# One encoder layer on one core: x loaded in the order of the turned tokens, the second pair of x tiles normed ahead of the parameters, constants fed to TensorE in its waits, expert 0's rows weighted later, the S5 matrix B built one chunk earlier

## The chip, the cores and the metric

One NeuronCore of a Trainium2 chip. Its engines run side by side and wait for each other by semaphores: TensorE (PE; its weight load is PEld), VectorE (DVE), ScalarE (ACT), GpSimd (POOL) and SyncE (SP), which here only issues DMAs; ACT and POOL issue some too. The metric is the device time of one execution in microseconds, the lower the better; the values of before are three runs.

## The reference

One layer over 512 tokens (an 8 x 64 grid) of width 1024, all float32:

```python
h = rms_norm(x, norm_mix)                      # x (512, 1024)
q, k, v, u, q_xa, gates = split(h @ w_in)      # w_in (1024, 5120)
x = x + (sum_b sigmoid(gate_b) * P_b(branch_b)) @ w_out
#   neighbourhood attention, 8 heads, 8 x 16 window on the grid, learned bias
#   bidirectional S5 scan (16 groups x 16 channels, 64 states), GELU, GLU
#   4-head cross-attention into 256 memory tokens, normed and projected
h2 = rms_norm(x, norm_ffn)
x = x + moe(h2)      # 4 groups x 4 experts, top-1 group, top-2 experts in it, FF 256
return rms_norm(x, final_norm)
```

The S5 step needs B-bar times the powers of the state's decay for each lag within a block of 8 tokens; before calls this ba. A token's two experts weight their outputs with softmax(top 2) times the group's probability.

## The kernel before

**Precision.** A product of two float32 matrices is three fp32r products: each operand is split into hi (rounded copy) and lo (rest), and `split()` (lines 1533 to 1537) adds hi x hi, lo x hi and hi x lo. A weight chunk arrives in `raw`, ScalarE writes w_hi (`hi`, L560), VectorE w_lo = raw - w_hi (`lo`, L962), then TensorE may take it. `RAW` = 6 raw buffers, `HL` = 2 pairs of w_hi and w_lo.

**Queues.** Each engine's program is written out in its own block and runs in order. SP issues every weight load in order of chunks; a load of chunk c waits until w_lo of chunk c - 6 is done.

**The opening.** SP loads x in four tiles of 128 tokens in natural order (L432), then chunk 0, the parameters (rows of the tile prm, L445, and the log step, L454), chunk 1, mem, chunks 2 and 3. ScalarE first loads its table for the square root (L571), then squares each tile with a sum (L574); after each pair the roots. VectorE turns them into 1/rms (`inverse_root`) and scales the tiles (`norm_x`, L970). TensorE transposes the normed tiles block by block (`turn`, L1557): eight blocks b of 128 columns, each block's 512 tokens in one PSUM bank, `TURN_BANK`. Blocks 0 to 5 are turned in two halves, (0, 1) and (2, 3), blocks 6 and 7 whole, after blocks 0 and 1 have left their banks. Between the halves stands `turn_params` (L1543), which turns prm into per-partition columns prt (the norm's gains among them); VectorE prepares prm for it (L977), after all eight parameter transfers, before it goes on to the second pair. From prt on, ScalarE writes h_hi = gain x block (`turn_hi`, L585) and VectorE h_lo (`turn_lo`, L988). The tokens are kept in another order from here on, column within the grid before row, so that both write with a stride of eight elements what they read in runs. The later load of x for the residual (L494) and the last sums already use that order: `every_eighth` writes 16 partitions, eight apart, of all four tiles, one transfer for each of the eight grid rows.

**Projection and branches.** Chunks c = 0 to 52 follow, with one to four products each (`product`), on banks 0 and 1 in turn. Chunks 0 and 1 give u of S5, 2 and 3 the cross-attention's queries, 4 to 7 the keys and values of mem, 8 to 19 q, k, v, 20 to 52 gates and branch projections. Work of the branches stands between the chunks on each engine at hand-placed values of c. On VectorE: `disc`, `powers` and `bbar` (c = 1 to 3) prepare B-bar, and `forward_b(h)`, called at c = 6 and 7 behind w_lo of chunk c + 2, multiplies it by powers for half of the states: four multiplies of 128 x 512 (L1078 to L1081; banks 2, 3 and 7, junk) and two sums into ba (L1083). `v_take` (L1195) copies turned values, for chunk 8 those of the memory (vm). TensorE turns values between the chunks (`turn_values`, L1670: the second of them, behind chunk 8's product, waits for v_take of the first), and ba from c = 9 on. GpSimd builds ba's other direction meanwhile.

**Routing and experts.** After w_out, the logits of the last tiles end on TensorE as products of 20 columns. VectorE picks groups and experts (`chosen`), TensorE sums their one-hots to places (`places`, L1847), VectorE builds one-hot tiles for the first `NHOT` = 4 experts, TensorE turns each into row numbers (L1859), and GpSimd gathers the rows of h2 by them into xg (L2148). For all experts GpSimd scatters token numbers and weights into tok_scratch (L2163, eight transfers), reads them back as idx (L2171) and copies each expert's weights to wcur (L2175); from expert 4 on it gathers by idx. `tokens(e)` (L1871) turns xg, `gate_up` multiplies by the gate and up weights in two halves, and the next step multiplies by the down weights (products `e_hi, at_hi`). An expert's weights are three units of 1 MB; ScalarE splits e_hi (`unit_hi`, L799), VectorE e_lo (L1413). ScalarE takes expert e - 1's output times its tokens' weights to ysb (`y_take(e)`, L855), which waits for wcur, and GpSimd adds it to the accumulator in DRAM (`add_y`, L413). For expert 0 ScalarE's y_take(1) stands in step 2, between unit 8's split and the tanh of expert 2; TensorE's down product of step 2 waits for it.

## Time and profile before

| | |
|---|---|
| runs of before (us) | 639.74, 641.40, 640.41; median 640.41 |
| profiled execution | 639.83 us, its span 638.2 us, mean granted clock 0.965 |
| PE busy in the span | 588.4 us (92%) |
| DVE, ACT, POOL busy | 416.5 (65%), 324.3 (51%), 221.4 (35%) us |

PE is busy in nearly all of the 40 slices of the page; the exceptions are the first and second, the end, and two around 450 and 485 us, where also the granted clock of TensorE is below 1 on average:

```profile
PE   2899799999999999999999999997497999999992
PEclk9899899999999999999999999997597999999997
```

Each digit is a slice of 16 us in tenths. A granted clock of 1.00 is 2.4 GHz, one of 0.50 is 1.2 GHz. In a timeline a matmul's duration counts until its end is modelled; the pace of a stream is the difference of two starts, or the length in the chain.

### The profile page before, as it was taken

The numbers are of one execution on the slowest core, as the hardware profiler recorded it, in microseconds if no ns is written. First come the engines' busy times: TensorE is split into PE (matmuls) and PEld (weight loads), VectorE is DVE, ScalarE is ACT, GpSimd is POOL, SyncE is SP. The second block draws the span as 40 slices with busy tenths as digits, with TensorE's granted clock in tenths as the row PEclk, the third lists the DMA queues.
The fourth block names the chain that finished last, engine by engine and source line by source line (L and its number), as shares of the span: only waits on it lengthen the run. The fifth ranks groups of instructions, "written<-read, shape, count | busy, mean of one in ns | idle before, by whom it ended". The sixth has DMA issues, their size and how long they took to land.

```text
span 638.2 us, 8989 instructions
## 1 busy us (share of the span) xinstructions
PE 588.4 (92%) x3149; PEld 477.0 (75%) x3149; DVE 416.5 (65%) x744; ACT 324.3 (51%) x533; POOL 221.4 (35%) x235
## 2 busy tenths in 40 slices
PE   2899799999999999999999999997497999999992
PEld 2688688889877777777677888887376888888871
DVE  3977523695376664554842379324877899999967
ACT  5866133222344433553243326315175998998853
POOL 3507985995000810000000000023665345434930
PEclk9899899999999999999999999997597999999997
DMA  9994523420253222222322336973599999999355
GB/s 299 197 217 115 116 68 101 126 72 1 63 169 88 78 66 67 67 67 66 100 65 67 100 99 155 334 275 132 158 324 405 374 365 393 399 386 374 130 108 199
DMA packets 89232, 111.46 MB, mean 175 GB/s; under 512 B 19647, under 2 KB 66913, under 8 KB 89192
## 3 DMA queue, kind: packets, MB, share of 16 engines
q1 hardware_dynamic: 79128, 93.65, 45.2%
q0 software_dynamic: 7280, 15.12, 8.7%
q10 hardware_dynamic: 2784, 2.18, 1.2%
q8 instruction: 23, 0.38, 0.2%
q14 instruction: 17, 0.14, 0.1%
HBM read 102.08 MB, written 14.75 MB: 183 GB/s over the span
## 4 chain that ended last, share of the span: by engine, by line
PE 77%; DVE 7%; DMA 5%; issue 4%; SPq 2%; POOL 2%; ACT 1%; POOLq 0%; ACTq 0%; DVEq 0%
PE bank L1535 21%; PE bank L1537 20%; PE bank L1536 20%; PE bank L1716 2%; PE bank L1690 2%; PE bank L1703 2%; DMA acc_scratch<-ysb,idx 2%; PE bank L1871 2%; DMA tok_scratch<-pay,rowi 1%; PE bank L1821 1%; SPq L483 1%; PE bank L1651 1%; DVE w_lo L962 1%; POOL tok_scratch L2163 1%; PE bank L1655 1%
## 5 line engine op out<-in xcount | busy, mean ns | idle before, releaser
L962 DVE TENSOR_TENSOR w_lo<-raw,w_hi 128x1024 fp32r<-128x1024 f32 x55 | 73.2, 1331 | 110.0 <-ACT w_hi L560 109.5
L1535 PE MATMUL bank<-h_hi,w_hi 128*128 128x512 f32 x320 | 129.6, 405 | 0.3 <-DVE w_lo L962 0.3
L1537 PE MATMUL bank<-h_hi,w_lo 128*128 128x512 f32 x320 | 126.1, 394 | 0.0
L1536 PE MATMUL bank<-h_lo,w_hi 128*128 128x512 f32 x320 | 125.6, 393 | 0.0
L1413 DVE TENSOR_TENSOR e_lo<-eraw,e_hi 128x2048 fp32r<-128x2048 f32 x48 | 108.7, 2291 | 8.9 <-ACT e_hi L799 7.6
L799 ACT CAST e_hi<-eraw 128x2048 fp32r<-128x2048 f32 x48 | 91.8, 1915 | 10.6 <-PE bank L1537 6.4
L560 ACT CAST w_hi<-raw 128x1024 fp32r<-128x1024 f32 x55 | 57.6, 1047 | 33.8 <-PE bank L1537 33.6
L1535 PEld LDWEIGHTS bank<-h_hi,w_hi 128*128 128x128 f32 x320 | 61.0, 191 | 13.1 <-DVE w_lo L962 0.9
L1537 PEld LDWEIGHTS bank<-h_hi,w_lo 128*128 128x128 f32 x320 | 60.6, 189 | 13.4
L1536 PEld LDWEIGHTS bank<-h_lo,w_hi 128*128 128x128 f32 x320 | 61.0, 191 | 11.7
L2113 POOL TENSOR_TENSOR wcf<-wcf,prt 128x160 f32<-128x160 f32 x1 | 0.5, 458 | 194.9 <-DMA wcf<-in_moe_w_fine 194.9
L1535 PE MATMUL bank<-e_hi,xt_hi 128*128 128x512 f32 x128 | 52.7, 412 | 1.6 <-DVE e_lo L1413 1.0
L1536 PE MATMUL bank<-e_lo,xt_hi 128*128 128x512 f32 x128 | 51.0, 398 | 0.0
L1537 PE MATMUL bank<-e_hi,xt_lo 128*128 128x512 f32 x128 | 51.0, 398 | 0.0
L413 POOL DMA_INDIRECT acc_scratch<-ysb,idx x14 | 25.6, 1831 | 56.8 <-PE bank L1871 41.6
L659 ACT ACTIVATE gt<-bank,bgh 128x512 f32<-128x512 f32 x24 | 16.5, 689 | 43.5 <-PE bank L1537 43.5
L2148 POOL DMA_INDIRECT xg<-h_scratch,idx x16 | 30.1, 1881 | 11.5 <-DVE idx L1408 8.6
L673 ACT ACTIVATE pr<-ssb,soft 128x192 f32<-128x192 f32 (+1 forms) x32 | 15.2, 475 | 30.2 <-DVE soft L1223 30.2
L1535 PE MATMUL bank<-e_hi,at_hi 128*128 128x512 f32 x64 | 26.1, 407 | 4.7 <-ACT ysb L855 3.7
L1535 PEld LDWEIGHTS bank<-e_hi,xt_hi 128*128 128x128 f32 x128 | 24.8, 193 | 7.3 <-DVE e_lo L1413 1.0
L1537 PEld LDWEIGHTS bank<-e_hi,xt_lo 128*128 128x128 f32 x128 | 24.6, 193 | 5.4
L1536 PEld LDWEIGHTS bank<-e_lo,xt_hi 128*128 128x128 f32 x128 | 24.8, 194 | 4.7
(390 smaller groups left out, 1228.5 us busy)
## 6 DMA issues: line engine op xcount, KB each, us to landing
raw<-in_w_in SPq DMA_DIRECT2D x40, 512.0 KB, 3.9
eraw<-in_moe_w_gate SPq DMA_DIRECT2D x32, 512.0 KB
eraw<-in_moe_w_up SPq DMA_DIRECT2D x32, 512.0 KB
eraw<-in_moe_w_down SPq DMA_DIRECT2D x32, 512.0 KB
raw<-in_w_out SPq DMA_DIRECT2D x8, 512.0 KB, 3.8
x_sb<-in_x SPq DMA_DIRECT2D x4, 512.0 KB, 5.0
raw<-in_w_mem_kv SPq DMA_DIRECT2D x4, 512.0 KB, 9.8
raw<-in_w_br_na SPq DMA_DIRECT2D x4, 512.0 KB, 3.4
```

The source lines that it names most:

```text
L413: pool.indirect_dma_start(out=acc_dram, out_offset=bass.IndirectOffsetOnAxis(ap=v(idx, 2 * e, [1, 1]), axis=0), in_=v(ysb, D * (e % 2), [1 ...
L560: act.copy(v(dst, o, [1, 1024]), v(raw, 1024 * (c % RAW), [1, 1024])).then_inc(sem("w_hi_done"), 1)
L659: ins = act.activation(v(gt, SEQ * m, [1, SEQ]), pv(g % 2, 0, [1, SEQ]), ACT.Tanh, scale=0.5, bias=v(bgh, KD * branch + m, [1, 1]))
L673: ins = act.activation(v(pr, 512 * (p % 2) + 256 * j, [1, n]), src, ACT.Exp, bias=v(soft, so + 1, [1, 1]), accum_out=v(soft, so + 2, [1, 1]))
L799: act.copy(v(e_hi[dst], 0, [1, 2048]), v(eraw[j], 0, [1, 2048])).then_inc(sem("e_hi_done"), 1)
L962: dve.tensor_tensor(v(l_, o, [1, 1024]), v(raw, 1024 * (c % RAW), [1, 1024]), raw32(v(h_, o, [1, 1024])), SUB).then_inc(sem("w_lo_done"), 1)
L1413: dve.tensor_tensor(v(e_lo[dst], 0, [1, 2048]), v(eraw[j], 0, [1, 2048]), raw32(v(e_hi[dst], 0, [1, 2048])), SUB).then_inc(sem("e_lo_done" ...
L1535: pe.matmul(dst, w[0], x[0], start=first, stop=False)
L1536: pe.matmul(dst, w[0], x[1], start=False, stop=False)
L1537: return pe.matmul(dst, w[1], x[0], start=False, stop=last)
L1690: ins = pe.matmul(pv(2 + j, 0, [1, n]), x, y, start=True, stop=True)
L2148: pool.indirect_dma_start(out=v(xg, D * (e % 3), [1, D]), out_offset=None, in_=h2_dram, in_offset=bass.IndirectOffsetOnAxis(ap=rows, axis= ...
```

## The change

x is loaded by 16 transfers of 128 KB, each of one grid row (16 partitions, eight apart) of two tiles: the even rows on SP, the odd rows on ACT ahead of everything else there, first those of tiles 0 and 1, then of 2 and 3. So tokens lie in their later order from the start and `turn_hi`, `turn_lo` read and write in runs; a square waits for all eight transfers of its pair. VectorE norms the second pair before it waits for the parameters. TensorE turns seven blocks of the first pair, then the same of the second, then the parameters, and waits for prt; block 6 has a bank of its own (bank 1), and only block 7 waits for a bank. `warm(b, n)` issues n bf16 products of a constant 128 x 128 by 512 columns into bank b, whose results nobody reads: 2 and 6 in the opening, 12 before `chosen`, (8, 0, 12, 1) ahead of the four one-hot tiles, 12 ahead of the first gathered rows, 3 behind their turning. y_take(1) takes expert 0's output unweighted and doesn't wait for wcur; `y_first`, in step 2 ahead of y_take(2), multiplies it in place, and add_y(0) waits for that. forward_b moves from c = 6, 7 to c = 5, 6.

```diff
 # loads, tile order
-        for n in range(NT):
-            sp.dma_start(v(x_sb, D * n, [1, D]), x_nat[:, n, :]).then_inc(sem(f"x_in{n}"), 16)
+        for n in (0, 2):
+            for r in range(0, ROWS, 2):
+                sp.dma_start(every_eighth(x_sb, r, n, 2), x_rows[:, n:n + 2, r, :]).then_inc(sem(f"x_in{n}"), 16)
...
+        for n in (0, 2):
+            for r in range(1, ROWS, 2):
+                act.dma_start(every_eighth(x_sb, r, n, 2), x_rows[:, n:n + 2, r, :]).then_inc(sem(f"x_in{n}"), 16)
         act.wait_ge(sem("stat_set"), 1)
         act.activation(v(stat, 40, [1, 1]), v(stat, 48, [1, 1]), ACT.Sqrt)
         for n in range(NT):
-            act.wait_ge(sem(f"x_in{n}"), 16)
+            if n % 2 == 0:
+                act.wait_ge(sem(f"x_in{n}"), 16 * ROWS)
...
-    TURN_BANK = (4, 5, 6, 7, 2, 3, 4, 5) + 2 * (4, 5, 6, 7)
+    TURN_BANK = (4, 5, 6, 7, 2, 3, 1, 4) + 2 * (4, 5, 6, 7)
...
-                act.activation(v(h_hi, SEQ * b, [1, ROWS], [ROWS, GW]), pv(TURN_BANK[b], 0, [GW, ROWS], [1, GW]),
-                               ACT.Identity, scale=pcol(GMIX + b)).then_inc(sem("turn_hi"), 1)
+                act.activation(v(h_hi, SEQ * b, [1, SEQ]), pv(TURN_BANK[b], 0, [1, SEQ]), ACT.Identity, scale=pcol(GMIX + b)).then_inc(sem("turn_hi"), 1)
...
         norm_x(0)
         norm_x(1)
+        inverse_root(2, 2, 2)
+        norm_x(2)
+        norm_x(3)
         dve.wait_ge(sem("prm_in"), 16 * 8)
         done(dve.tensor_copy(v(prm, 0, [64, 2], [1, 64], p0=LDT, pn=DP),
                              v(stat, 60, [1, 2], [0, 64], p0=LDT, pn=DP)), "prm_ready")
-        inverse_root(2, 2, 2)
-        norm_x(2)
-        norm_x(3)
...
         for b in range(6):
             turn(b, (0, 1))
+        turn(6, (0, 1))
+        warm(0, 2)
+        for b in range(7):
+            turn(b, (2, 3))
         turn_params()
-        for b in range(6):
-            turn(b, (2, 3))
-        for b in range(6, KD):
-            turn(b, (0, 1, 2, 3))
+        pe.wait_ge(sem("prt_ready"), 1)
+        warm(0, 6)
+        turn(7, (0, 1, 2, 3))
 # B
-            if c in (6, 7):
+            if c in (5, 6):
                 dve.wait_ge(sem("ct_ready"), 2)
-                forward_b(c - 6)
-            if c == 7:
+                forward_b(c - 5)
+            if c == 6:
                 dve.sem_inc(sem("ba_ready"), 1)
 # constants
+        def warm(b, n):
+            for _ in range(n):
+                pe.matmul(pv(b, 0, [1, 512]), v(onesb, 0, [1, P]), v(onesb, 0, [0, 4], [1, P]), start=True, stop=True)
...
         logits(3)
+        warm(0, 12)
         pe.wait_ge(sem("chosen"), 1)
...
         for e in range(NHOT):
+            warm(0, (8, 0, 12, 1)[e])
             pe.wait_ge(sem("hot"), e + 1)
...
+        warm(0, 12)
         pe.wait_ge(sem("rows"), 1)
         tokens(0, 0, 16)
+        warm(0, 3)
 # expert 0's rows
-            act.wait_ge(sem("wcur"), e)
+            plain = isinstance(e, int) and e == 1
+            if not plain:
+                act.wait_ge(sem("wcur"), e)
...
-                                     ACT.Identity, scale=v(wcur, 0 if odd else 1, [1, 1]))
+                                     ACT.Identity, scale=1.0 if plain else v(wcur, 0 if odd else 1, [1, 1]))
...
+        def y_first():
+            act.wait_ge(sem("y_a"), 1)
+            act.wait_ge(sem("wcur"), 1)
+            act.mul(v(ysb, 0, [1, D]), v(ysb, 0, [1, D]), v(wcur, 0, [1, 1])).then_inc(sem("y_first"), 1)
```

## Rows read from the trace of the kernel before

**Rows 1.** timeline, 0 to 22 us: start, us, engine, operation, line, [idle before <-releaser]

```profile
0.93 1.28 ACT L571 ACT_TABLE_LOAD   x1 [0.93 <-PEq L2228]
...
4.33 1.06 ACT L574 ACTIVATE squares<-x_sb 128x1024 f32<-128x1024 f32 x1 [1.90 <-DMA x_sb<-in_x]
...
9.51 2.79 PE L1557 MATMUL bank<-ident,x_sb 128*128 128x128 f32 x12 [9.51 <-DVE x_sb L970]
...
12.13 0.22 DVE L977 COPY prm<-stat 16x128 f32<-16x128 f32 x1 [2.76 <-DMA stat<-in_s_log_dt]
...
14.71 1.53 PE L1557 MATMUL bank<-ident,x_sb 128*128 128x128 f32 x12 [1.89 <-DVE x_sb L970]
14.86 1.23 DVE L962 TENSOR_TENSOR w_lo<-raw,w_hi 128x1024 fp32r<-128x1024 f32 x1
15.25 7.87 ACT L585 ACTIVATE h_hi<-bank,prt 128x512 fp32r<-128x512 f32 x8 [3.64 <-PE bank L1557]
...
16.50 6.47 DVE L988 SCALAR_TENSOR_TENSOR h_lo<-bank,prt,h_hi 128x512 fp32r<-128x512 f32 x6 [0.42 <-ACT h_hi L585]
```

**Rows 2.** timeline, TensorE, around the second product and around 71 us

```profile
26.46 0.50 PE L1535 MATMUL bank<-h_hi,w_hi 128*128 128x512 f32 x1
...
71.24 0.66 PE L1670 MATMUL bank<-ident,vt 128*128 128x128 f32 x2 [3.87 <-DVE vm L1195]
```

**Rows 3.** timeline, VectorE, 54 to 73 us

```profile
55.03 1.85 DVE L962 TENSOR_TENSOR w_lo<-raw,w_hi 128x1024 fp32r<-128x1024 f32 x1 [0.20 <-ACT w_hi L560]
59.59 1.96 DVE L962 TENSOR_TENSOR w_lo<-raw,w_hi 128x1024 fp32r<-128x1024 f32 x1 [2.72 <-ACT w_hi L560]
61.48 0.68 DVE L1078 TENSOR_TENSOR bank<-pw,bank 128x512 f32<-128x512 f32 x1
...
65.30 1.51 DVE L962 TENSOR_TENSOR w_lo<-raw,w_hi 128x1024 fp32r<-128x1024 f32 x1
...
70.67 0.42 DVE L1195 COPY vm<-bank 128x256 f32<-128x256 f32 x1 [0.15 <-DVE ba L1083]
```

**Rows 4.** waits of TensorE, whole span: waiter <- releaser: total us, times, longest

```profile
PE bank L1859 <- DVE hot L1401: 5.6, 4, 2.8
```

**Rows 5.** timeline, routing and first experts

```profile
445.82 0.23 PE L1847 MATMUL bank<-selb,upper 128*128 128x64 bf16 x1 [2.88 <-DVE selb L1381]
...
455.78 1.94 PE L1871 MATMUL bank<-ident,xg 128*128 128x128 f32 x8 [2.90 <-DMA xg<-h_scratch,idx]
...
487.23 1.06 POOL L2148 DMA_INDIRECT xg<-h_scratch,idx  x1 [0.15 <-issue]
...
488.46 0.76 PE L1535 MATMUL bank<-e_hi,at_hi 128*128 128x512 f32 x1 [3.66 <-ACT ysb L855]
...
496.91 1.05 PE L1871 MATMUL bank<-ident,xg 128*128 128x128 f32 x8
```

**Rows 6.** windows: us, busy us of each engine, granted clock, DMA share, GB/s

```profile
3.50:8.50 5.00, 0.00 (x0) 0.00 (x0) 1.40 (x6) 3.51 (x6) 3.32 (x6) 1.00 0.98 362
391.00:401.00 10.00, 10.00 (x46) 8.28 (x45) 7.89 (x8) 6.49 (x8) 0.00 (x0) 1.00 1.01 235
442.00:444.00 2.00, 0.94 (x5) 0.83 (x4) 0.98 (x8) 1.98 (x2) 0.00 (x1) 0.50 0.67 270
490.00:492.00 2.00, 2.00 (x6) 1.52 (x5) 1.59 (x1) 0.37 (x1) 2.00 (x2) 0.50 1.04 414
```

**Rows 7.** chain that ended last, around 72 us: start, us, what

```profile
72.33 0.43 PE bank L1536
...
75.40 0.23 PE bank L1536
```

**Rows 8.** instructions on tile x_sb, the later load: ns min/median/max

```profile
L494 SPq DMA_DIRECT2D x_sb<-in_x x8: 580/595/701, 390.1 to 394.7; - x8
```

**Rows 9.** groups by line and form, VectorE, 100 to 360: busy us, mean ns

```profile
L1183 DVE SCALAR_TENSOR_TENSOR merged<-gt,bank 128x512 f32<-128x512 f32 x8 | 5.5, 684 | 3.5 <-PE bank L1537 3.3 <-DVE merged L1183 0.2
```

**Rows 10.** DMA queues, 492 to 493 us: packets, MB, share of 16 engines

```profile
q0 software_dynamic: 85, 0.09, 25.6%
```

More of the change, by code:

```diff
@@ L129, in v, with every_eighth @@
         return bass.AP(tensor=first.tensor, offset=first.offset + off, ap=[first.ap[0]] + [list(d) for d in dims])
-    def every_eighth(t, r):
+    def every_eighth(t, r, n0=0, nn=NT):
         first = t[r:r + 1, 0:1]
-        return bass.AP(tensor=first.tensor, offset=first.offset, ap=[[ROWS * first.ap[0][0], P // ROWS], [D, NT], [1, D]])
+        return bass.AP(tensor=first.tensor, offset=first.offset + D * n0,
+                       ap=[[ROWS * first.ap[0][0], P // ROWS], [D, nn], [1, D]])
     def spread(t, r, cols):
@@ L284, in build @@
     x_rows = a["x"][0].rearrange("(r n c) d -> c n r d", r=ROWS, n=NT)
-    x_nat = a["x"][0].rearrange("(n p) d -> p n d", p=P)
     out_nat = out[0].rearrange("(n p) d -> p n d", p=P)
@@ L406, in add_y @@
     def add_y(pool, e):
-        pool.wait_ge(sem("y_a"), e + 1)
+        if e == 0:
+            pool.wait_ge(sem("y_first"), 1)
+        else:
+            pool.wait_ge(sem("y_a"), e + 1)
         if e == 0:
@@ L894, in step @@
             elif not peeled or 2 <= e < 15:
+                if peeled and e == 2:
+                    y_first()
                 y_take(e, odd)
@@ L986, in turn_lo @@
             if b < KD:
-                o = [[1, ROWS], [ROWS, GW]]
-                dve.scalar_tensor_tensor(v(h_lo, SEQ * b, *o), pv(TURN_BANK[b], 0, [GW, ROWS], [1, GW]),
-                                         pcol(GMIX + b), raw32(v(h_hi, SEQ * b, *o)), MUL, SUB).then_inc(
+                dve.scalar_tensor_tensor(v(h_lo, SEQ * b, [1, SEQ]), pv(TURN_BANK[b], 0, [1, SEQ]),
+                                         pcol(GMIX + b), raw32(v(h_hi, SEQ * b, [1, SEQ])), MUL, SUB).then_inc(
                                              sem("turn_lo"), 1)
@@ L1510, in last_sum @@
             dve.wait_ge(sem("out_k"), NT + n + 1)
-            dve.wait_ge(sem(f"x_in{n}"), 48)
+            dve.wait_ge(sem(f"x_in{n}"), 32 if n % 2 else 32 + 16 * ROWS)
             for b in range(2):
@@ L1549, in turn @@
                 pe.wait_ge(sem("normed"), tiles[-1] + 1)
-                if b >= 6:
-                    pe.wait_ge(sem("turn_lo"), b - 5)
+                if b == 7:
+                    pe.wait_ge(sem("turn_lo"), 1)
             else:
```

## The prediction

> **What bounds the kernel now.** I read the waits of TensorE first, then the order of time around each, then the windows and the chain. Outside three places TensorE hardly waits, so the change pays only there. The first is the opening: TensorE's first instruction stands at 9.51, because x has to land, be squared and be normed; the second pair of x tiles is then held up by VectorE, which waits 2.76 us for the parameters; and from 15.25 on ScalarE and VectorE take eight turned blocks out of PSUM, 7.87 us for eight and 6.47 for six [rows 1], before w_lo of chunk 1 and the second product at 26.46 [rows 2]. The second is one stall: at 71.24 TensorE has idled 3.87 us for VectorE's copy of vm [rows 2], which stood behind forward_b [rows 3]. The third is routing with the first experts, where TensorE waits 5.6 us in four pieces for the one-hot tiles [rows 4], 2.88 for the chosen experts, 2.90 for the first gathered rows and 3.66 for ScalarE's ysb [rows 5]. After such a stretch the granted clock is 0.50 (1.2 GHz) for a while, as at 442 to 444 and 490 to 492 [rows 6]; products then follow each other every 0.43 us and not every 0.23 [rows 7].
>
> **Opening: x by 16 transfers, second pair ahead of the parameters.** Removed: the 2.76 us wait. Added: 12 more DMA issues, eight of them on ScalarE ahead of its table load. An issue of this kind, for a transfer twice as big, took 0.595 us [rows 8]; the bounds for one are 0 and 0.7, and I take 0.6. So ScalarE issues until 0.93 + 8 x 0.6 = 5.7 and, with the table load of 1.28 [rows 1] and the small root of 0.2 (an estimate), squares from 7.2, not from 4.33. First pair: 2.9 late, first transpose at 12.4 instead of 9.51.
>
> Landing: each new transfer writes 16 partitions eight apart. The nearest rows are the later loads of x of the same form, 235 GB/s for the core while they ran, against 362 in the opening now [rows 6]. Half a MB at 362 is 1.45 us and the first tile was in use at 4.33, so 2.9 us go beside the data. 2.1 MB at 235 is 8.9: second pair there at 11.8. From first square to first transpose it took 9.51 - 4.33 = 5.2, so transposes of the second pair start at 17.0, not at 14.71 [rows 1]. Fourteen of them now stand ahead of the parameters' transpose: 14 x 0.13 (12 took 1.53) = 1.8, then 0.7 for it and its copy (an estimate): prt is ready at 19.5 and h_hi starts 4.2 us later than at 15.25.
>
> What comes back is the eviction. The block in PSUM is now in its final order, so it is written contiguously; VectorE's nearest instruction of that size takes 0.68 [rows 9] against 6.47 / 6 = 1.08. VectorE: w_lo of chunk 0 1.2, eight h_lo 5.4, w_lo of chunk 1 1.2, end 27.3. TensorE: six constants, block 7 at 21.5, then 24 x 0.23 = 5.5 us of first product, end 27.5. The second product starts there and not at 26.46: **1.0 us lost**. From the other side: with loads at full rate ScalarE binds (first pair squared at 9.7, transposes of the second at 14.9), the end is 25.2 and 1.2 are gained; with 0.23 a transpose in both pairs (the first twelve took 2.79) and 3.4 us of the first product at half speed, 4.1 are lost. I stay at 1.0, since the form of the transfer is that of the 235 row. SP issues the parameters about 3 us later, behind eight transfers instead of four; they were there at 12.1, so about 15, in time for the norm's end at about 17. The chunks and mem behind them shift as far, hidden while ScalarE is on h_hi, which even now it leaves only at 23.1.
>
> The Trainium skill, page SBUF — State Buffer, section Door 1: The DMA port swizzle, says that a transfer reaches only the ports its partitions map to, all 16 only if it spans all 128. By its formula the partitions of one new transfer lie on 8 ports, an estimate of 218 GB/s, by which 1.7 us would be lost in place of 1.0; the 235 measured agrees roughly.
>
> **B one chunk earlier.** forward_b's instructions are only moved, from behind chunks 6 and 7 to behind 5 and 6. w_lo of chunk 7 ends at 55.03 + 1.85 = 56.9; forward_b takes 65.30 - 61.48 = 3.8, to 60.7; w_lo of chunk 8 1.7 (between 1.51 and 1.96), to 62.4 instead of 61.55 [rows 3]. So product 8 starts 0.9 late and ends at 68.3 (now 71.24 - 3.87 = 67.4). The second half runs to 66.2, w_lo of chunk 9 to 67.7, vm is copied by 68.1: just in time. TensorE goes on at 68.3 in place of 71.24, 2.9 less. With the idle time the half clock goes too: six products at 0.43 instead of 0.23 [rows 7] and two transposes of 0.66 in place of 0.25 [rows 2], 1.6. Together **4.5 gained**; 2.9 if the clock falls anyway, 0 if vm waits as before (rival 6). Behind it TensorE waits for next to nothing as far as 400 us, so it is kept. Late next is w_lo of chunk 8.
>
> **Constants in routing.** They stand in order on TensorE, so each group is free only if it ends before that which it is put ahead of. No row shows a bf16 product of 512 columns; the nearest are the products of 512 at 0.23 and 0.43. Twelve start at 445.82 - 2.88 = 442.9 [rows 5], the clock at 0.50 [rows 6]. At full speed 12 x 0.23 = 2.8 us just fill the wait; at half they take 5.2 and end 2.3 late. Near 72 us the clock came back after about 3.4 us of unbroken work: 72.33 is slow, 75.40 fast [rows 7]. So eight slow and four fast, end 447.3, 1.5 late, part of which VectorE's own work hides. The next 8 + 12 + 1 are 4.8 us against 5.6 of waits [rows 4], the last 12 2.8 against 2.90. I take 1.2 us of delay for all that hangs on routing: 0 if it never runs at half, 8 in rival 5. In return the first experts' products run at 0.23: twelve save 2.4, of which VectorE's e_lo, next to be late, leaves about 1.6.
>
> **First rows weighted later.** The 3.66 us wait for ysb goes, and the slow stretch behind it (0.50 at 490 to 492 [rows 6]), 13 products, 2.6. ScalarE takes the rows as soon as it has split unit 8, for which TensorE still waits about 1.3; y_first adds a 1024-column multiply before the next take (1.06 by the squares' row), hidden. Late next is the gather for expert 4: issued at 487.23 [rows 5], behind the arrival of idx, which this edit doesn't move, and now behind 1.2 us of constants. GpSimd's queue was still moving bytes at 492 to 493 [rows 10]; I put its landing at 493.3 now and 494.6 after. TensorE would be ready at about 492, and turns the rows at 494.6 in place of 496.91 [rows 5]: 2.3 gained, less 0.7 for a chance of 4 in 10 that 2.7 us of idling halve the clock for 3.4 us (1.7). **1.6 gained.** Bounds: if the gather lands only at 496.5 now, 2.6 are lost (0.9 late, 1.7 clock); if it is never late, 5.0 are gained.
>
> **Sum.** +1.0 - 4.5 - 1.6 = -5.1. The profiled execution took 639.83 (638.2 of span, 1.6 around it), so 634.7; it lies 0.6 under the median of the runs, so 635.3.
>
> **Rivals.**
> 1. The gather of expert 4 is early and the experts gain 5.0 instead of 1.6: 631.9. For: no row shows its landing. Against: the queue's late bytes. 0.15.
> 2. That gather gives the gain back, +2.6 in place of -1.6: 639.5. For: the core's DMA is full of weights there. 0.19.
> 3. The opening costs 4.1 and not 1.0: 638.4. For: the second pair then falls on slow transposes. Against: the constants. 0.10.
> 4. The opening gains 1.2: 633.1. For: the 235 stands for a stretch with other transfers in it. 0.11.
> 5. Slower: the constants never lift the clock, so 12, 8, 12, 1 and 12 of them run at 0.43. The places come 2.3 us late; 21 more take 9.0 against 5.6 of waits, the last 12 5.2 against 2.9: about 8 us on the first gathered rows and on the chain to idx, in place of 1.6 gained: 644.9. It decides if the granted clock is still 0.50 behind the first twelve. Against: near 72 us unbroken work brought it back. 0.05.
> 6. B earlier doesn't do what it says: vm still waits, behind a stretched w_lo, and 4.5 shrinks to 0: 639.8. Against: forward_b is the only work between. 0.04.
>
> The forecast has 0.36 (its own range 633.2 to 637.5). What a measurement can't tell from no change is within 0.3%, 1.9 us, of 640.41. Faster: forecast, 1, 4, two thirds of 3, a third of 2: 0.75. Same: 6 and most of the rest of 2 and 3: 0.18. Slower: 5 and a tail of 2: 0.07. Range 631.0 to 640.3.
>
> **What would show it.** Opening: first square near 7.2, second pair landed near 11.8, h_hi from 19.5 at 0.6 each, second product near 27.4. Middle: no idling above 2 us between 58 and 75, granted clock 1.00 there. Routing: clock 1.00 within 4 us of the first constants, first gathered rows turned about 1.2 late. Experts: waits for ysb under 2 us and a new wait for the gather of expert 4. I am wrong above all if x lands whole by 9 us, if the one-hots wait for constants, or if that gather comes later than 496.

## The result: 651.0 us, slower than before

| | us |
|---|---|
| before, 5 runs | 639.74 to 642.72, median 640.41 |
| after, 5 runs | 643.81 to 654.89, median 651.0 |
| ratio of after to before | 1.013, 95% interval 1.0085 to 1.0174 |
| predicted | 635.3 (631.0 to 640.3) |
| after's profiled execution | 643.81, span 642.2, granted clock 0.983 |

The forecast had the wrong sign. The ratios, here and below, leave out runs that are over 1.5% above the fastest of their kernel, as they may be in a slower state of the chip (here 654.89). The runs spread over 11 us and the profiled execution is the fastest of the five, so its trace shows only part of the loss. On the page TensorE's row is better than before at the first weak place (9 for 4) and its clock row at both (9 for 5 and for 7), yet the chain that ended last no longer runs over TensorE alone:

```profile
PE   1898999999999999999999999999987999999980
...
PEclk9999999999999999999999999997999999999995
...
PE 54%; DMA 21%; DVE 10%; issue 6%; ACT 3%; POOL 3%; SPq 2%; POOLq 0%; ACTq 0%; DVEq 0%
DMA acc_scratch<-ysb,idx 17%; PE bank L1550 14%; PE bank L1552 13%; PE bank L1551 13%; DVE w_lo L978 2%; PE bank L1736 2%; PE bank L1723 2%; PE bank L1710 2%; DMA xg<-h_scratch,idx 1%; POOL tok_scratch L2190 1%; PE bank L1671 1%; PE bank L1
```

Before, that chain was 77% PE, and the transfer `acc_scratch<-ysb,idx`, by which GpSimd adds an expert's output to the accumulator in DRAM, had 2% of it. It has 17% now.

**Up to expert 4 it goes much as forecast.** The opening in the timeline of after (start, duration, engine, line, operation; answers to [rows 1]):

```profile
0.94 5.18 ACTq L576 DMA_DIRECT2D x_sb<-in_x  x8
...
8.19 1.06 ACT L582 ACTIVATE squares<-x_sb 128x1024 f32<-128x1024 f32 x1 [0.55 <-DMA x_sb<-in_x]
...
12.86 1.06 ACT L582 ACTIVATE squares<-x_sb 128x1024 f32<-128x1024 f32 x1 [2.15 <-DMA x_sb<-in_x]
...
17.67 1.75 PE L1577 MATMUL bank<-ident,x_sb 128*128 128x128 f32 x14 [1.09 <-DVE x_sb L986]
...
19.91 4.74 ACT L593 ACTIVATE h_hi<-bank,prt 128x512 fp32r<-128x512 f32 x8 [3.60 <-DVE prt L999]
...
21.06 5.36 DVE L1003 SCALAR_TENSOR_TENSOR h_lo<-bank,prt,h_hi 128x512 fp32r<-128x512 f32 x8
```

ScalarE issues for 5.18 us, the first square stands at 8.19, h_hi starts at 19.91 and takes 0.59 a block, h_lo 0.67 [rows 1, 9]. The second product starts at 27.88, 1.42 late. While x was loaded, the core moved 223 GB/s (last number of the window), where before moved 362:

```profile
3.50:8.50 5.00, 0.00 (x0) 0.00 (x0) 0.00 (x0) 1.80 (x3) 3.32 (x6) 1.00 1.00 223
```

The middle and the S5 outputs on TensorE (answers to [rows 2]):

```profile
70.06 0.41 PE L1690 MATMUL bank<-ident,vt 128*128 128x128 f32 x2 [0.23 <-DVE vm L1210]
...
147.50 0.49 PE L1671 MATMUL bank<-st_re,ca 128*128 128x128 f32 x2 [0.84 <-DVE st_im L1147]
```

The wait for vm is 0.23 us and the granted clock 1.00 from 55 to 80. At 80 us after is 2.63 us ahead. At 147.50 TensorE waits for S5's state, which VectorE doesn't have earlier; 1.1 us go back there.

Routing and the first experts on TensorE (answers to [rows 5]), then three windows of after (us, busy of each engine, granted clock, DMA share, GB/s):

```profile
440.44 5.29 PE L1558 MATMUL bank<-onesb 128*128 128x512 bf16 x12
...
454.93 1.14 PE L1896 MATMUL bank<-ident,xg 128*128 128x128 f32 x8
...
478.87 1.16 PE L1896 MATMUL bank<-ident,xg 128*128 128x128 f32 x8 [1.36 <-DMA xg<-h_scratch,idx]
...
483.68 0.47 PE L1550 MATMUL bank<-e_hi,at_hi 128*128 128x512 f32 x1 [0.90 <-ACT ysb L864]
...
492.08 1.15 PE L1896 MATMUL bank<-ident,xg 128*128 128x128 f32 x8 [2.45 <-DMA xg<-h_scratch,idx]
```

```profile
441.00:446.00 5.00, 5.00 (x21) 1.91 (x19) 3.27 (x19) 1.98 (x3) 0.00 (x0) 0.51 0.26 105
446.00:452.00 6.00, 5.25 (x36) 2.29 (x35) 5.76 (x13) 0.00 (x0) 2.24 (x1) 1.00 0.00 0
484.00:488.00 4.00, 4.00 (x19) 3.29 (x18) 3.90 (x4) 2.83 (x2) 2.11 (x3) 1.00 1.03 411
```

The first twelve constants all ran at the half clock, 5.29 us for twelve, and only behind them the granted clock is back at 1.00. TensorE came to the places at 445.51; VectorE had written the chosen experts (selb) by 443.4. The stall for ysb is 0.90 in place of 3.66, and tokens(4) waits 2.45 us for its gather: 492.08 in place of 496.91, 4.8 us ahead of before.

**Behind that, everything is given back.** ScalarE around the first add of after, then the first and the twelfth add on GpSimd:

```profile
482.45 1.09 ACT L864 ACTIVATE ysb<-bank 128x512 f32<-128x512 f32 x2
...
488.59 1.15 ACT L871 ACTIVATE ysb<-ysb,wcur 128x1024 f32<-128x1024 f32 x1
```

```profile
490.55 2.00 POOL L416 DMA_INDIRECT acc_scratch<-ysb,idx  x1 [4.29 <-ACT ysb L871]
...
596.48 2.81 POOL L416 DMA_INDIRECT acc_scratch<-ysb,idx  x1 [4.86 <-DMA acc_scratch<-ysb,idx]
```

The same two adds, the first and the last steady one, of before:

```profile
489.13 1.67 POOL L413 DMA_INDIRECT acc_scratch<-ysb,idx  x1 [0.84 <-ACT ysb L855]
...
591.22 2.00 POOL L413 DMA_INDIRECT acc_scratch<-ysb,idx  x1 [5.92 <-DMA acc_scratch<-ysb,idx]
```

y_take(1) runs at 482.45, but y_first stands behind the splits of two units, at 488.59, and the first add waits for it: 490.55, where before had 489.13. From there the chain of after is one add behind the other (start, length, what):

```profile
490.55 9.12 DMA acc_scratch<-ysb,idx
...
500.53 8.73 DMA acc_scratch<-ysb,idx
...
510.11 8.65 DMA acc_scratch<-ysb,idx
```

An add waits until the one before has landed. How GpSimd came to its 14 adds, first before, then after (durations of the issue in ns, min/median/max; idle us and times by what ended them):

```profile
L413 POOL DMA_INDIRECT acc_scratch<-ysb,idx x14: 1577/1724/2196, 489.1 to 611.6; - x14
...
  PE bank L1871: 41.6, 9
  DMA acc_scratch<-ysb,idx: 14.2, 3
```

```profile
L416 POOL DMA_INDIRECT acc_scratch<-ysb,idx x14: 1577/2186/3554, 490.6 to 615.5; - x14
...
  DMA acc_scratch<-ysb,idx: 63.8, 12
```

Before, TensorE's progress released nine of the fourteen adds and a landing three. After, the landing of the add before released twelve. Eleven steps from 490.55 to 596.48 are 9.63 us each, against TensorE's own 9.31 an expert; before they were (591.22 - 489.13) / 11 = 9.28. So the last steady add is 5.3 us late, 1.4 by its start and 3.8 by the pace. Of that the tail gives some back and takes some more: the next add follows after 10.8 us and not 14.2, but its issue takes 3.49 us, not 1.62. The loads of the accumulated rows, which wait for the adds, start 4.0 us late, first before, then after, and that is the difference of the two spans:

```profile
616.94 4.98 SPq L545 DMA_DIRECT2D xf<-acc_scratch  x8
```

```profile
620.91 4.99 SPq L549 DMA_DIRECT2D xf<-acc_scratch  x8
```

TensorE was not what came late: at the last `tokens` of this stretch it still led before by 1.0 us (598.26 against 599.28). It had lost 3.8 of its 4.8 us, as GpSimd's program has, for each expert, a copy to wcur, the gather for a later expert and one add in turn, so that late adds hold up gathers: between 484 and 606 TensorE waits three times for gathered rows, 3.8 us with the 2.45 above, in before not once.

### The profile page after: what moved, and what is told of

It reads as the page before. It is cut to its first block, busy times and chain, and to the rows that moved or that the text cites. A ratio compares the mean times of both kernels' runs of the same rounds, so it can differ in the third digit from the quotient of the medians.

```text
span 642.2 us, 9113 instructions
## 1 busy us (share of the span) xinstructions
PE 594.9 (93%) x3205; PEld 475.4 (74%) x3205; DVE 414.4 (65%) x744; ACT 321.7 (50%) x534; POOL 213.4 (33%) x235
## 4 chain that ended last, share of the span: by engine, by line
PE 54%; DMA 21%; DVE 10%; issue 6%; ACT 3%; POOL 3%; SPq 2%; POOLq 0%; ACTq 0%; DVEq 0%
DMA acc_scratch<-ysb,idx 17%; PE bank L1550 14%; PE bank L1552 13%; PE bank L1551 13%; DVE w_lo L978 2%; PE bank L1736 2%; PE bank L1723 2%; PE bank L1710 2%; DMA xg<-h_scratch,idx 1%; POOL tok_scratch L2190 1%; PE bank L1671 1%; PE bank L1844 1%; SPq L487 1%; DMA x_sb<-in_x 1%; PE bank L1558 1%
## 5 line engine op out<-in xcount | busy, mean ns | idle before, releaser
L978 DVE TENSOR_TENSOR w_lo<-raw,w_hi 128x1024 fp32r<-128x1024 f32 x55 | 74.7, 1358 | 106.2 <-ACT w_hi L564 105.5
L1550 PE MATMUL bank<-h_hi,w_hi 128*128 128x512 f32 x320 | 128.2, 401 | 1.6 <-DVE w_lo L978 1.6
L416 POOL DMA_INDIRECT acc_scratch<-ysb,idx x14 | 33.0, 2359 | 68.2 <-DMA acc_scratch<-ysb,idx 63.8
L854 ACT CAST xt_hi<-bank 128x512 fp32r<-128x512 f32 x32 | 17.2, 591 | 20.6 <-PE bank L1896 20.4
```

Of the source, the lines that this page charges most:

```text
L416: pool.indirect_dma_start(out=acc_dram, out_offset=bass.IndirectOffsetOnAxis(ap=v(idx, 2 * e, [1, 1]), axis=0), in_=v(ysb, D * (e % 2), [1 ...
L854: act.copy(v(xt_hi[odd], 512 * j, [1, 512]), pv(4 + j, 0, [1, 512])).then_inc(sem("xt_hi"), 1)
L978: dve.tensor_tensor(v(l_, o, [1, 1024]), v(raw, 1024 * (c % RAW), [1, 1024]), raw32(v(h_, o, [1, 1024])), SUB).then_inc(sem("w_lo_done"), 1)
L1550: pe.matmul(dst, w[0], x[0], start=first, stop=False)
```

## Experiments

Theory: expert 0's late weighting sets off a serial chain of adds that was at its limit already. Each kernel was compared with runs of before on the same chip (medians 640.8 to 641.6); "ratio" is to those, with its 95% interval. "Less than after" is against its median of 651.0; a second series of after (after_again, below) had 648.36, which makes each such difference 2.6 us smaller.

### Undoing y_first, moving it, breaking the chain

**a_weighted**: after, with

```diff
-            plain = isinstance(e, int) and e == 1
-            if not plain:
-                act.wait_ge(sem("wcur"), e)
+            act.wait_ge(sem("wcur"), e)
...
-                if peeled and e == 2:
-                    y_first()
```

`scale` and add_y's wait are as in before again, too.

> After with one part undone: y_take(1) weights expert 0's rows again and waits for wcur, y_first is gone. Theory (chain of adds): the adds to the accumulator run one after the other, each 8.8 us to landing and 0.86 to the next start, which is more than TensorE's 9.31 us per expert, so the last steady add stands at the first plus 11 x 9.6 and the end follows it. Here the first add moves from 490.55 to about 486.5 (wcur at 484.3, two takes of 0.6, the start of the DMA), TensorE stalls 2 us more at about 484: end 4 us earlier than after's profiled 643.8, about 640. Rival 1 (the loss of after sits before the experts, in the opening or the constants): no change but the stall, 645 to 648. Rival 2 (the DMA engines are full in the experts, so every period is 9.6 whatever starts when): within 1 us of 643.8 or later.

Measured 639.04, ratio 0.9954 (0.9932 to 0.9976): 12 us less than after by taking one part out. The stall is back (3.7 us for ysb); the first add stands at 486.84.

**a_two_acc**: after, with odd adds to a second tensor. The kernel leaves the rows of that tensor out of its output, so it is a probe and no candidate; the waits of y_take and of the last loads, not shown, follow the two semaphores.

```diff
-        pool.indirect_dma_start(out=acc_dram,
+        pool.indirect_dma_start(out=acc2_dram if e % 2 else acc_dram,
...
-            pool.wait_ge(sem("y_acc"), 16 * e)
+            pool.wait_ge(sem(("y_acc", "acc_set")[e % 2]), 16 * (e // 2) + (48 if e % 2 else 0))
```

> After, with the adds of the odd experts sent to a second DRAM tensor (filled from x beforehand), so that each add waits only for the last but one; the second tensor is left out of the output. Theory (chain of adds): TensorE runs at its own 9.31 us per expert from tokens(4) at 492.08, the last steady add at about 586.5 in place of 596.48: 10 us less, about 634, and the spread of the runs falls to that of before (3 us). Rival (DMA engines full): the period stays at 9.6 and the time within 2 us of after's 643.8. Rival (only the phase of GpSimd's descriptors against VectorE counts): the adds still take 2.2 us to issue, but without a chain this costs nothing, so it would look as under the theory; the issue times tell it apart.

Measured 635.61 (635.21 to 637.23), 0.9906 (0.9878 to 0.9934): 15 us less than after, and the spread is 2 us. The DMA engines are as busy as ever (share 1.00 from 500 to 600, 0.98 in after), so it was not their fill. Steady adds now follow each other every 9.31 us, though each takes 2.1 to issue.

**a_early**: after, with y_first one unit earlier.

```diff
                 unit_hi(3 * e + 3, (n0 + 1) % EU, load_of(n0 + 1, i), 0)
+                if peeled and e == 2:
+                    y_first()
                 unit_hi(3 * e + 4, (n0 + 2) % EU, load_of(n0 + 2, i), 1)
```

> After, with y_first placed behind the split of unit 9 and not behind that of unit 10, 3 us earlier on ScalarE. Theory (chain of adds): the first add moves from 490.55 to about 487.6, every later add with it, TensorE unchanged until tokens(4): 3 us less than 643.8, about 641. Rivals (loss before the experts; DMA engines full): no change, 643 to 645.

Measured 642.14, 1.0000 (0.9973 to 1.0026). More than the 3 us came back, yet it is 3 us slower than a_weighted, though both start alike. First and last steady add on GpSimd, of a_weighted and of a_early:

```profile
486.84 1.67 POOL L413 DMA_INDIRECT acc_scratch<-ysb,idx  x1 [0.83 <-ACT ysb L859]
...
587.66 2.09 POOL L413 DMA_INDIRECT acc_scratch<-ysb,idx  x1 [3.65 <-ACT ysb L859]
```

```profile
486.98 2.00 POOL L416 DMA_INDIRECT acc_scratch<-ysb,idx  x1 [1.21 <-ACT ysb L871]
...
595.99 2.23 POOL L416 DMA_INDIRECT acc_scratch<-ysb,idx  x1 [5.08 <-DMA acc_scratch<-ysb,idx]
```

Steps of 9.17 there, 9.91 here. So the start is not all. In a_weighted TensorE has lost 3.7 us to the stall and turns expert 4's rows at 493.47, in a_early at 491.59: the same adds stand further behind TensorE in a_early, and twelve adds wait for a landing, where in a_weighted five do. That a landing releases the adds doesn't make them slow by itself: it releases twelve in the profiles of b_B, b_open, b_const and b_split too, with steps of 9.39 to 9.50. What counts is how long a step is, and the next part takes it to pieces.

**b_yfirst**: before, with y_first alone (the part of the change as in its diff).

> Before, with the one part: expert 0's rows taken unweighted, weighted by y_first ahead of y_take(2). Theory (chain of adds): TensorE's stall of 3.66 us goes, but y_first stands some 6 us behind y_take(1), so the first add moves from 489.13 to about 492; with adds back to back at 9.6 the end comes 3 (TensorE's pace kept) to 7 us later: 643 to 647. As I predicted for this part: 1.6 us gained, 638.8. Rival (loss sits in the opening or the constants): between 636 and 640.

Measured 655.04, 1.0191 (1.0155 to 1.0227): by itself this part costs 12 us by the ratio and 13.5 by the medians, more than the theory's 7 and, by the medians, more than the whole change (the intervals of the two ratios overlap). Its first ten steps are 9.3 to 12.5 us.

### Why the steps get longer

VectorE and GpSimd around the fifth add of after:

```profile
528.64 4.49 DVE L1428 TENSOR_TENSOR e_lo<-eraw,e_hi 128x2048 fp32r<-128x2048 f32 x2
```

```profile
528.84 3.55 POOL L416 DMA_INDIRECT acc_scratch<-ysb,idx  x1 [5.10 <-DMA acc_scratch<-ysb,idx]
```

The two e_lo run from 528.64 to 530.93 and from 530.84 to 533.13. The issue of the add starts 0.2 us into the first and ends at 532.39, 1.46 behind that one's end. The same 1.46 to 1.48 us stand behind the end of a running e_lo in ten other adds of after and in seven of before; where none runs at its start, the issue takes 1.58 to 1.67, also beside VectorE's instructions that read a PSUM bank. The Trainium skill, page SBUF — State Buffer, section SBUF: two separate sides, states that VectorE and GpSimd share a port pair by an exclusive lock held for a whole instruction, and that a VectorE instruction with two SBUF inputs, as e_lo is, takes it against a GpSimd instruction that reads SBUF. The trace agrees that GpSimd waits for the end of e_lo; it adds that 1.46 us of the issue still lie behind it. What exactly of the issue is held up no run shows. In a_weighted the issues take 1.59 us each from 496 to 532 and 2.1 from 541 on, where TensorE paces them; in after, where each starts by the landing of the one before, they take 1.7 to 3.6.

A step is the issue, the rest of the transfer up to its landing, and the time to the next add. Summed over the eleven steps from the first add to the last steady one (us, from rows like those above; the runs not yet named follow below):

| | issues | issue's end to landing | landing to next add | eleven steps |
|---|---|---|---|---|
| before | 20.4 | 71.6 | 10.1 | 102.1 |
| after | 25.2 | 71.5 | 9.3 | 105.9 |
| after_again | 26.6 | 71.3 | 9.3 | 107.1 |
| a_late_pe | 23.2 | 70.9 | 9.3 | 103.4 |
| a_esplit | 24.3 | 72.7 | 9.3 | 106.3 |
| b_B | 24.5 | 70.1 | 9.3 | 103.9 |
| b_yfirst | 27.8 | 75.4 | 9.3 | 112.6 |
| a_oldopen | 27.5 | 79.0 | 9.3 | 115.7 |

In the two profiles of after the transfers take what they took before; the longer issues, 4.7 and 6.1 us, more than make up the slower pace, 3.8 and 5.0. In b_yfirst and a_oldopen the transfers are longer too.

**a_late_pe**: after, with more work on TensorE.

```diff
         for e in range(3):
             step(e)
+            if e == 2:
+                warm(7, 24)
```

> After, with 24 more constants (5.5 us of work that nobody reads) on TensorE behind step 2; nothing else. The first add stays at 490.55, tokens(4) comes about 3 us later than 492.08. Theory (chain of adds and its phase): the issue of an add ends 1.46 us after VectorE's running e_lo (2.29 us) ends, so adds that start by the landing of the one before, wherever VectorE is, take 2.4 us to issue, and adds that TensorE paces take 1.6 to 2.1; with TensorE later the adds are paced by it again, each step falls from 9.6 to 9.3, the last steady add stands near 592 in place of 596.5 and the kernel gets 3 to 5 us faster than after (651.0 median), 646 to 648, although it has 5.5 us more work. Rival (chain alone, no phase): the adds keep 9.6 and the time is after's, 650 to 652. Rival (TensorE's work is what counts): 3 us slower, 654.

Measured 643.45, 1.0027 (1.0003 to 1.0052): 7.5 us less than after. The 24 products and tokens(4) on TensorE, then the last steady add:

```profile
486.37 5.35 PE L1558 MATMUL bank<-onesb 128*128 128x512 bf16 x24
...
494.52 1.05 PE L1896 MATMUL bank<-ident,xg 128*128 128x128 f32 x8
```

```profile
593.75 2.35 POOL L416 DMA_INDIRECT acc_scratch<-ysb,idx  x1 [2.30 <-DMA acc_scratch<-ysb,idx]
```

The adds stayed a chain of landings (twelve waits of 36.6 us in all, 63.8 in after), with a shorter step, 9.40, most of it by shorter issues (23.2 in place of 25.2 us). Against after_again's median the gain is 4.9 us. That 5.35 us of useless work make the kernel faster speaks against TensorE's own work as the cause; that TensorE took over the pace was wrong.

**a_esplit**: after, with shorter instructions on VectorE.

```diff
-            dve.tensor_tensor(v(e_lo[dst], 0, [1, 2048]), v(eraw[j], 0, [1, 2048]),
-                              raw32(v(e_hi[dst], 0, [1, 2048])), SUB).then_inc(sem("e_lo_done"), 1)
+            for o in (0, 1024):
+                ins = dve.tensor_tensor(v(e_lo[dst], o, [1, 1024]), v(eraw[j], o, [1, 1024]),
+                                        raw32(v(e_hi[dst], o, [1, 1024])), SUB)
+            ins.then_inc(sem("e_lo_done"), 1)
```

> After, with each e_lo (128 x 2048 on VectorE, 2.29 us) made by two instructions of 1024 columns. Theory (phase): an add's issue then waits for at most 1.2 us of a running instruction instead of 2.29; the issues fall from 2.35 us in the mean to 1.9 or less, the chain's step by 0.45, eleven steps 5 us: about 646 against 651. Rival (the issue's length has nothing to do with VectorE's instruction): issues stay at 2.35 and the time at 651, or 0.2 us more per expert where VectorE is the bound: 653.

Measured 638.85, 0.9946 (0.9918 to 0.9975): 12 us less than after, but not as worked out. The issues fell only to 2.23 in the mean (after: 2.36; the median rose from 2.19 to 2.26), the steps of the profiled execution stayed at 9.66, and the first add came 2.8 us earlier. That is most of what the two profiled executions differ by (640.46 and 643.81); the rest of the 12 us no trace shows. GpSimd got to the gather of expert 3 at 466.10, not 469.37, and through the copies to wcur by 479.1, not 485.1; TensorE and ScalarE were then 2.7 us ahead, and with them y_first (485.83, not 488.59). So what shortens is GpSimd's way through the routing. **b_split** shows the same, before with this edit alone:

> Before with e_lo by two instructions of 1024 columns alone. Theory (GpSimd's work waits for VectorE's running instruction, in the scatters, in the copies to wcur and in the adds): the first add moves 2 to 3 us forward, as from 484.37 to 481.70 with B and the constants, the late adds get shorter: 3 to 5 us less than before, 0.993 to 0.995. Rival (the split only helps a kernel whose TensorE is ahead): 1.000.

Measured 635.32 (634.52 to 638.55), 0.9918 (0.9890 to 0.9946). The third and fourth scatter of token numbers, before and b_split:

```profile
459.03 3.08 POOL L2163 DMA_INDIRECT tok_scratch<-pay,rowi  x1 [0.30 <-issue]
462.41 1.90 POOL L2163 DMA_INDIRECT tok_scratch<-pay,rowi  x1 [0.30 <-issue]
```

```profile
459.88 0.97 POOL L2165 DMA_INDIRECT tok_scratch<-pay,rowi  x1 [0.31 <-issue]
461.15 1.96 POOL L2165 DMA_INDIRECT tok_scratch<-pay,rowi  x1 [0.30 <-issue]
```

A scatter that meets no e_lo takes 0.97. The first add moves from 489.13 to 486.38; the steps get no shorter (9.39, before 9.28). So the gain is in the way to the first add and, 2.1 us, behind the last steady one.

**b_two_acc**: before, with a_two_acc's edit.

> Before, with the adds of the odd experts sent to a second DRAM tensor that is left out of the output. Theory (in before TensorE sets the pace, and the adds, 8.3 us to landing and 0.86, have only 0.16 us of room): hardly faster, 0 to 1.5 us below before (640.9), with a smaller spread. Rival (the chain of adds bound before too): over 4 us faster, as in the changed kernel, where it gave 15 us.

Measured 636.16, 0.9921 (0.9893 to 0.9949), 4.7 us less: the rival's number. So the chain of adds bounds before too, in part, and my 0.16 us of room were none. Before's profiled execution has three adds that waited for a landing; its longer runs (up to 649.7 beside this one) may have more, which no trace of before shows. b_const, below, which is as fast as before in the median, has twelve in a profiled execution of 645.02.

### The other parts

**b_B**: before with `if c in (5, 6)`, `forward_b(c - 5)` alone.

> Before, with forward_b at c = 5, 6 alone. TensorE's start of product 8's successors at 80 us is 3.9 us earlier in after than the opening alone would have it (1.25 late at 40 us, 2.63 early at 80 us). Theory (chain of adds): the adds' chain starts from the routing, so it moves with everything else; nothing is taken back: 3.9 us less than before, a ratio of 0.994. Rival: the wait for S5's state at 147 us, which took 1.1 us back in after, belongs to this part: 2.8 us less, 0.9956. Rival (the DMA queue sets the end whatever starts when): 1.000.

637.51, 0.9938 (0.9915 to 0.9962). The interval holds both numbers. By the trace the rival is right on the place: a wait of 0.7 us for S5's state is in it.

**b_open**: before with the opening alone.

> Before, with after's opening alone (x by 16 transfers, second pair ahead of the parameters, contiguous evictions, the 8 constants of the opening). From after's trace: second product at 27.88 in place of 26.46, 1.25 us late at 40 us, kept to the end: ratio 1.002. As I predicted for it: 1.0 us late. Rival (the opening is what made after slow, by later parameters): over 3 us, 1.005 and more.

643.03, 1.0048 (1.0019 to 1.0077), 2.2 us by the medians, 3.1 by the ratio; the interval does not decide between 1.3 and the rival's 3.

**b_const**: before with the constants in routing alone.

> Before, with the constants in routing and ahead of the first experts alone. Theory (chain of adds): the first add hangs on chosen, the scatter and idx, which the constants make about 0.5 us later (idx came 1.9 us earlier in after's routing than before where the logits ended 2.4 earlier); TensorE gains some 3 us in experts 0 to 2 and gives them back in the wait for ysb, which grows from 3.7 to over 5: end 0 to 1 us later, 1.000 to 1.0015. Rival (constants gain what TensorE shows at tokens(1), 2.8 us): 0.9955. Rival (constants are after's loss): 1.005 and more.

641.24, 1.0003 (0.9983 to 1.0023), as expected. The profiled execution was a long one, 645.02.

**c_Bconst**: before with B earlier and the constants.

> Before, with B one chunk earlier and the constants, without the opening and without y_first. Theory: 3.9 gained and 0.5 lost: 3.4 us less than before, 0.9947, first add at about 485.7. Rival (constants gain too): 0.990. Rival (only together do parts lose, by the phase in which the adds meet VectorE's splits): 1.000 and more, with adds whose issue takes over 2 us.

637.33, 0.9950 (0.9925 to 0.9975), as expected: it beats both kernels, by B alone. Its first add stood at 484.37, 1.3 earlier than expected.

**a_oldopen**: after without its opening.

> After without its opening (before's loads, norms and evictions of x), with B earlier, the constants and y_first. The opening alone cost 1.0048 of before on its own. Theory: its cost adds up with the rest, so 2 to 3 us less than after: 648 to 649, still slower than before. Rival (the opening makes the loss, by the moment at which everything meets GpSimd): 641 or less.

647.41, 1.0081 (1.0046 to 1.0116). The parts add up roughly. Its profiled execution, 652.26, was one of its longest (the fastest took 642.13) and shows what a single bad one looks like (chain, start and length of adds):

```profile
508.55 11.02 DMA acc_scratch<-ysb,idx
...
520.42 8.96 DMA acc_scratch<-ysb,idx
...
530.22 10.28 DMA acc_scratch<-ysb,idx
```

**after_again**: after, unchanged.

> After, unchanged, to see by another profile where the 7 us go by which its median (651.0) stands above the profiled execution (643.8). Theory (chain of adds and its phase): the first add stands at 490 to 491 again and the steps between adds are longer, 10 us and more, with issues of 2.5 to 3.5 us; the time stays near 651. Rival (the extra time lies before the experts): the first add is late.

648.36 (644.28 to 652.59), 1.0124 (1.0079 to 1.0169). The profiled execution took 645.19, again one of the fastest, with the first add at 490.12 and steps of 9.74, so the question stayed open: no profile shows after at 651. Its steps are 0.1 us longer than those of the execution at 643.81, all of it in the issues, and a_oldopen's bad execution has steps of 10.5; both point to the steps between adds, and neither shows it for after.

**c_split**: c_Bconst with e_lo in two.

> Before, with B one chunk earlier, the routing constants and e_lo by two instructions of 1024 columns: a candidate for the fastest. In the version without the split (637.3) TensorE paces most adds, so the theory gives it little: 0 to 1.5 us less (the late adds, those of 2.1 to 2.2 us, get shorter), 636 to 637.3. Rival (VectorE becomes the bound with 0.1 to 0.2 us more per expert): 638 to 640.

632.26 (630.90 to 632.79), 0.9847 (0.9811 to 0.9882): 8.5 us below before, the fastest here, and 4 to 5 us better than expected. First add, then TensorE's tokens(4) and (5), then VectorE in a steady stretch:

```profile
481.70 1.67 POOL L413 DMA_INDIRECT acc_scratch<-ysb,idx  x1 [0.30 <-issue]
```

```profile
487.38 1.15 PE L1880 MATMUL bank<-ident,xg 128*128 128x128 f32 x8 [0.69 <-DMA xg<-h_scratch,idx]
...
496.79 1.05 PE L1880 MATMUL bank<-ident,xg 128*128 128x128 f32 x8
```

```profile
540.00:590.00 50.00, 50.00 (x249) 41.96 (x248) 49.34 (x60) 45.01 (x49) 25.38 (x18) 1.00 1.01 376
```

The first add stands 7.4 us ahead of before's, and the steps are 9.09 us, with issues of 1.59 in the next five adds, all released by landings. VectorE is busy for 49.34 of 50 us: the dearer split didn't bind yet, but it is at its end.

## Why the prediction was wrong

- **Opening, 1.0 lost.** Right in mechanism, 1.4 in size: first square 8.19 (predicted 7.2), second pair squared from 12.86 (11.8), transposes 17.67 (17.0), h_hi 19.91 (19.5), second product 27.88 (27.4). x came at 223 GB/s, where 235 had been taken, and ScalarE's issues took 0.65 each, not 0.6. Alone the opening cost 2.2 by the medians.
- **B, 4.5 gained.** 3.9 at 80 us (from 1.25 late to 2.63 early), of which 1.1 went back at 147 us. "Behind it TensorE waits for next to nothing" was read from waits of a TensorE that came later; an engine that is not waited for in before can be late for one that arrives earlier. The kernel with B alone has -3.4 by the medians.
- **Constants, 1.2 of delay and a fast clock behind.** "Eight slow and four fast" was wrong: all twelve ran at 0.43 us each, the granted clock was 0.50 up to 445.7 and 1.00 from 446 on, over 5 us behind the first of them and not within 4. The places came 2.1 us late; tokens(0) came 0.85 early where 2.4 of lead had come into routing, so 1.5 of delay were left. That this is near 1.2 is in part luck. Rival 5 is false, but its first step, twelve constants at the half clock, came true: the clock rose just behind them, and the next 8 took 1.93 us, the next 12 2.75.
- **The gather of expert 4 next.** It was late by 2.45 us, as argued; tokens(4) came 4.8 ahead of before, where my steps gave 5.8 (4.5 for B and 2.3 here, less 1.0).
- **The step that failed** is one clause: "y_first adds a 1024-column multiply before the next take (1.06 by the squares' row), hidden." It is hidden from ScalarE and TensorE, and the first add stands right behind it. I asked what is late next for TensorE only, and took the period of 9.31 behind expert 4 as given. GpSimd's rows would have spoken: 8.2 us from issue to landing in the median, about 0.86 to the next issue, so 9.1 of 9.31, with three adds already released by a landing. In after the late first add is 1.4 of the 5.3 us by which the last steady add is late, the longer steps are 3.8. No rival held it; that the gain was "given back" stood only for a gather. Nor would the three signs named as "wrong above all" have told: x was whole at 12.8, the one-hots waited at most 0.4 us for constants, expert 4's rows were turned at 492.08. All three watch what TensorE needs. Without this step the forecast's other terms give -3.5; the kernel without it, a_weighted, measured -2.5 by the medians.
- The size: after is 7 to 11 us above before; y_first gives 12 to 13.5 (a_weighted, b_yfirst), the opening 2.2, the constants 0.4, B -3.4. These sum to 11 to 13, so the parts add up only roughly.

**Open.** Why one execution's steps are 9.6 and another's over 10: in a_oldopen's the transfer itself, behind the issue, takes 7.0 to 8.6 us in ten of eleven steps, where before's takes 6.1 to 7.5. No run here tells what it meets there; b_yfirst, which lost more than the theory's 7 us, has longer transfers too. Nor does a run set only the place at which the adds meet e_lo: that this place makes the issues long is shown add by add, that a lag behind TensorE leads to the bad places is argued from a_early and a_late_pe. Why the spread falls so far in c_split is only argued: its adds have some room again.

## What to carry to other kernels

When an edit takes a wait from the engine that bounds the kernel, follow what else hung on that wait: list every serial chain beside it (issue, landing, restart) and divide its step by the period; one at 98% of it is a second bound, and what starts it must not move back. If GpSimd is in such a chain, look at VectorE's instruction lengths before looking at GpSimd. And where runs spread over 11 us, one profile is a sample and can be the fastest of them: don't take what it shows for the whole difference.

## What the runs showed of the hardware

- GpSimd's indirect add takes 1.59 us to issue when no e_lo runs at its start, and up to 3.68 when it starts in an e_lo of 2.29 us (585.24 in a_early): it ends 1.46 to 1.48 us behind that e_lo. VectorE's instructions that read a PSUM bank don't hold it up (517.85 in before: 1.59, in an xt_lo). Scatters take 0.97 and up to 3.08. Halving the e_lo instructions took 5 us from before (b_split), though VectorE got no less work.
- An add of up to 128 rows of 4 KB to DRAM landed 7.7 to 9.7 us after its start beside weight loads in before (DMA share 1.03 from 540 to 590), up to 11.7 in b_yfirst, and 5.2 to 5.4 in before's tail without them. The Trainium skill, page DMA: Bandwidth & Descriptors, section Two DMAs through the same engine are not ordered, says that only the completion semaphore orders dependent transfers; this kernel keeps to it, and the price beside the loads was 8.5 (c_split) to 12.5 us (b_yfirst) per link.
- x by 16 transfers of 16 partitions each was whole for the first pair by about 8.1 us and for the second by 12.8, at 223 GB/s; four plain ones, at 362, had let the last square start at 8.94.
